# Delta rule with key and query norms folded into per-token factors, and decay rows spread by transfers from memory instead of products

## What is computed

```
q = repeat(l2norm(q), 2) * 128 ** -0.5      # 8 key heads of 128, 16 value heads
k = repeat(l2norm(k), 2)
gc    = cumsum(g)                            # per chunk of 64 tokens
decay = exp(gc[i] - gc[j])                   # j <= i
lhs   = eye + (beta_i k_i . k_j) * decay * (1 - eye)
u, w  = solve(lhs, v * beta), solve(lhs, k * beta * exp(gc))
attn  = (q_i . k_j) * decay
# per chunk: v_new = u - w S;  o = (q exp(gc)) S + attn v_new
#            S = S exp(gc_last) + (k exp(gc_last - gc))^T v_new
o = delta(forward) + reversed(delta(reversed inputs))
o = rms(o) * norm_w * silu(z);  y = o @ w_out
```

## Time and profile before

| | us |
|---|---|
| median of 3 runs | 1308.56 (1308.28 to 1309.36) |
| the profiled execution's own time | 1311.29 |
| its span in the profile | 1309.8 |
| PE busy | 1123.8 (86%) |
| DVE busy | 370.3 (28%) |
| ACT busy | 363.0 (28%) |
| POOL busy | 48.8 (4%) |
| mean granted clock of PE | 0.907 |

### The profile page before, as it was taken

The page is one execution under the profiler, slowest core; times in us unless marked ns, Lnnn a source line. Parts: engine busy times, 40 slices in busy tenths (PEclk is TensorE's granted clock), DMA queues, the critical chain, the costliest instruction groups (busy, mean ns, idle before and its releaser), DMA issues.

```text
span 1309.8 us, 23489 instructions
## 1 busy us (share of the span) xinstructions
PE 1123.8 (86%) x10332; PEld 852.1 (65%) x10332; DVE 370.3 (28%) x879; ACT 363.0 (28%) x902; POOL 48.8 (4%) x55
## 2 busy tenths in 40 slices
PE   6799999999889869767775979999997989996668
PEld 5577777777667654233332868888886877864457
DVE  1455655565442231000003124220002000614310
ACT  2345554655543111000003031120014011225220
POOL 1110010000000000000000000000000000400000
PEclk9799999999989969888886969999998998997559
DMA  5421221122011689999994224434441354430000
GB/s 209 185 100 66 91 75 67 67 92 74 35 66 65 280 367 407 420 421 421 422 421 193 97 100 146 159 111 147 161 160 65 101 189 115 177 129 1 0 1 33
DMA packets 35529, 210.55 MB, mean 161 GB/s; under 512 B 4688, under 2 KB 9168, under 8 KB 11488
## 3 DMA queue, kind: packets, MB, share of 16 engines
q1 hardware_dynamic: 35424, 209.00, 41.6%
HBM read 207.91 MB, written 1.08 MB: 160 GB/s over the span
## 4 chain that ended last, share of the span: by engine, by line
PE 72%; SPq 10%; DVE 6%; ACT 5%; DMA 4%; issue 2%; PEld 0%; PEldq 0%; ACTq 0%; DVEq 0%
PE ps L245 15%; SPq L230 10%; PE ps L397 10%; PE ps L1894 8%; PE ps L1812 4%; PE ps L400 4%; PE ps L698 2%; PE ps L709 2%; DMA arena<-in_wu 2%; PE ps L460 2%; PE ps L2225 2%; PE ps L426 2%; PE ps L445 2%; PE ps L261 1%; PE ps L1375 1%
## 5 line engine op out<-in xcount | busy, mean ns | idle before, releaser
L245 PE MATMUL ps<-slots,xt 128*128 128x256 f32 x640 | 139.1, 379 | 0.7 <-ACT xt L272 0.7
L397 PE MATMUL ps<-xt,slots 128*128 128x256 f32 x512 | 132.5, 407 | 2.0 <-DMA slots<-in_wu 2.0
L245 PEld LDWEIGHTS ps<-slots,xt 128*128 128x128 f32 x640 | 121.4, 190 | 17.8 <-ACT xt L272 1.1
L397 PEld LDWEIGHTS ps<-xt,slots 128*128 128x128 f32 x512 | 99.3, 202 | 26.7 <-issue 10.3
L1894 PE MATMUL ps<-slots,xt 128*128 128x256 f32 x512 | 110.7, 379 | 0.0
L1894 PEld LDWEIGHTS ps<-slots,xt 128*128 128x128 f32 x512 | 97.2, 190 | 13.2
L1375 PE MATMUL ps<-arena 128*32 128x512 f32 x304 | 48.9, 696 | 17.7 <-DMA arena<-in_wu 10.6
L400 PE MATMUL ps<-slots,arena 128*128 128x256 f32 x256 | 63.1, 389 | 0.0
L245 PE MATMUL ps<-slots,yt 128*128 128x256 f32 x256 | 57.8, 390 | 0.9 <-ACT yt L275 0.9
L1812 PE MATMUL ps<-xt,slots 128*128 128x256 f32 x256 | 58.1, 391 | 0.0
L989 DVE SCALAR_TENSOR_TENSOR arena<-arena 128x256 f32<-128x256 f32 x128 | 56.7, 489 | 0.3
(11 more groups left out here) (353 smaller groups left out, 1592.0 us busy)
## 6 DMA issues: line engine op xcount, KB each, us to landing
slots<-in_wu SPq DMA_DIRECT2D x120, 1024.0 KB, 4.9
arena<-in_wu SPq DMA_DIRECT2D x56, 1024.0 KB, 26.5
yt<-in_wu SPq DMA_DIRECT2D x10, 1024.0 KB, 26.2
arena<-bias_rows SPq DMA_DIRECT2D x1, 2048.0 KB, 15.6
arena<-in_xp SPq DMA_DIRECT2D x2, 512.0 KB, 4.4
xt<-in_xt SPq DMA_DIRECT2D x2, 512.0 KB, 9.2
x<-in_x SPq DMA_DIRECT2D x1, 1024.0 KB, 17.1
arena<-in_ln_g SPq DMA_DIRECT2D x2, 512.0 KB, 14.6
```

Source lines behind the costliest of these rows:

```text
L245: q = M.matmul(self.bank(cg, UC, t * UC), lhs[:, h * KT + k, t * P:(t + 1) * P], self.slot(s)[:, k, :], start=(t == 0 and k == 0 and h == ...
L397: q = M.matmul(bank(n, T), self.slots[:, s, k, n * P:(n + 1) * P], self.xt[:, k, :], start=(k == 0), stop=(k == KT - 1))
```

## The change

Four things are done at once.

1. Keys and queries stay unnormalised (`silu` writes them straight into `g.cv`). ACT squares them (`square`). `unit_sums` becomes four products with one column of ones, so that each token gets its sum on its own partition: 128x1 instead of 128x512.
2. The key norm goes into per-token numbers: `sums` (DVE) copies the sums, `unit` (ACT) takes the logarithm of two columns, `rates` (DVE) subtracts it from the logarithms of beta and decay, and `decay` and `scale_keys` use the result as bias and scale; `keep_v` scales the values by the key's length. The query norm goes into the epsilon of the output norm (`epsq`, `out_ln`).
3. The decay rows come by transfers: PE turns the summed gates once, ACT copies them (`g.crow`), SP stores them to a DRAM tensor `delta_rows` (two transfers), waits for that, and reads them back per head into `g.rowsb`, each row repeated over 64 partitions (two transfers a head). `decay_rows` and `spread` are gone.
4. `bars` waits for those transfers. `rates` waits for the logarithm on ACT.

```diff
@@ gdn_sync
         self.fill(0, U_GDN + 6)
+        SP.wait_ge(*g.cum_kept(1))
+        for x in range(2):
+            SP.dma_start(self.delta_rows[x].rearrange("c h (v i) -> (c h v) i", v=REP),
+                         g.crow[0:64, x * 64:(x + 1) * 64]).then_inc(*g.rows_out.up())
+        SP.wait_ge(*g.rows_out(2))
+
+        def rows_in(h):
+            for x in range(2):
+                SP.dma_start(g.rowsb[h % 2][g.halves[x]].rearrange("p (c n) -> p c n", c=4),
+                             self.delta_rows[x:x + 1, :, h, :].to_broadcast([P // 2, 4, P])).then_inc(
+                    *g.rows_in[h % 2].up())
+
+        rows_in(0)
+        rows_in(1)
         for h in range(QKH):
+            if h + 2 < QKH:
+                SP.wait_ge(*g.barred(h + 1))
+                rows_in(h + 2)
             self.fill(1, U_GDN + 3 * h + 4 if h + 1 < QKH else U_GOUT + 1)
@@ gdn_tensor
-        def decay_rows(h):
-            M.wait_ge(*g.spread(h + 1))
...
-            M.matmul(bank(2), c["together"], g.D[:, :, :, :].rearrange("p a b i -> p (a b i)"), start=True,
-                     stop=True).then_inc(*g.rows.up())
...
         def unit_sums(h):
+
             M.wait_ge(*g.squared(h + 1))
-            M.wait_ge(*g.barred(h + 1))
-            M.matmul(bank(2), c["ones"], g.sq[:, :, :].rearrange("p z t -> p (z t)"), start=True, stop=True).then_inc(
-                *g.unit_sums.up())
+            if h > 0:
+                M.wait_ge(*(g.sums_kept(1) if h == 1 else g.v_kept(h - 1)))
+            for cc in range(2):
+                for z in range(2):
+                    q = M.matmul(bank(2, 1, 2 * cc + z), g.sq[:, z, tile(cc)], c["ones"][:, 0:1], start=True, stop=True,
+                                 skip_group_check=True)
+            q.then_inc(*g.unit_sums.up())
...
         def keys(h):
             cv = g.cv[h % 3]
-            M.wait_ge(*g.unit(h + 1))
+            M.wait_ge(*g.qk_silu(h + 1))
...
-        decay_rows(0)
+        M.wait_ge(*g.gate_kept(1))
+        M.transpose(self.ps[0:64, 7, 0:P], g.cum[:, :, :, :].rearrange("p c w h -> p (c w h)"), ident).then_inc(
+            *g.cum_turned.up())
...
-            if ahead:
-                decay_rows(h + 1)
@@ gdn_scalar
         def silu(h):
             A.wait_ge(*g.qk_conv(2 * h + 2))
-            A.activation(g.cn[:, 0:2], g.cn[:, 0:2], ACT.Silu).then_inc(*g.qk_silu.up())
+            if h > 2:
+                A.wait_ge(*g.reads(3 * (h - 3) + 3))
+            for cc in range(2):
+                q = A.activation(g.cv[h % 3][:, :, cc * P:(cc + 1) * P].rearrange("p z (x i) -> p z x i", x=2),
+                                 self.chunks(g.cn[:, 0:2], cc), ACT.Silu)
+            q.then_inc(*g.qk_silu.up())
+
+        def square(h):
+            A.wait_ge(*g.qk_silu(h + 1))
+            if h > 0:
+                A.wait_ge(*g.unit_sums(h))
+            A.activation(g.sq[:, :, :], g.cv[h % 3][:, :, :], ACT.Square).then_inc(*g.squared.up())
...
         def unit(h):
 
             n = h - 3
-            A.wait_ge(*g.unit_sums(h + 1))
-            if h > 0:
-                A.wait_ge(*g.unit(h))
+            A.wait_ge(*g.sums_kept(h + 1))
             A.preload_act_table_set("natural_log_exp_and_others")
-            A.activation(g.rn[:, :, :], two(2), ACT.Ln, bias=col(0)).then_inc(*g.norm_ln.up())
+            A.activation(g.lnk[:, h], g.kss[:, h], ACT.Ln, bias=col(0)).then_inc(*g.norm_ln.up())
...
+            A.wait_ge(*g.rated(h + 1))
+            ss = g.rates[:, h, :, 2:4, :]
+            A.activation(ss, ss, ACT.Exp).then_inc(*g.rates_made.up())
@@ gdn_vector
         def bars(h):
-            V.wait_ge(*g.rows(h + 1))
+            V.wait_ge(*g.rows_in[h % 2](2 * (h // 2) + 2))
...
+        def sums(h):
...
+            V.wait_ge(*g.unit_sums(h + 1))
+            both = bank(2, 4).rearrange("p (c z) -> p c z", c=2)
+            V.tensor_copy(g.kss[:, h], both[:, :, 1])
+            V.tensor_scalar(g.epsq[:, h], both[:, :, 0], 1e-6 * HD, 1e-12 * HD, ALU.mult, ALU.add).then_inc(
+                *g.sums_kept.up())
+
+        def rates(h):
+            V.wait_ge(*g.norm_ln(h + 1))
+            V.tensor_tensor(g.rates[:, h], g.logs[:, :, :, 2 * h:2 * h + 2],
+                            g.lnk[:, h].unsqueeze(2).unsqueeze(3).to_broadcast([P, 2, 4, REP]), ALU.subtract).then_inc(
+                *g.rated.up())
...
         bars(0)
-        squares(0)
-        apply_unit(0)
+        sums(0)
+        rates(0)
         triangles(0)
```

More of the change, by code:

```diff
@@ L286, in gdn @@
         g.g, g.lb = al("g", [P, 2, 2, VH]), al("lb", [P, 2, 2, VH])
-        g.cum, g.egc, g.neg, g.bias, g.ss = (al(n, [P, 2, 2, VH]) for n in ("cum", "egc", "neg", "bias", "ss"))
+        g.cum, g.egc, g.neg = (al(n, [P, 2, 2, VH]) for n in ("cum", "egc", "neg"))
+        g.logs, g.rates = al("logs", [P, 2, 4, VH]), al("rates", [P, QKH, 2, 4, REP])
+        g.lnk, g.invk, g.epsq, g.kss = (al(n, [P, QKH, 2]) for n in ("lnk", "invk", "epsq", "kss"))
+        g.crow = al("crow", [P, P])
+        g.rowsb = [al(f"rows{b}", [P, 512]) for b in range(2)]
         g.eg = al("eg", [P, 2, 2, 2, VH])
@@ L311, in gdn @@
             new("SP", n, 16) for n in ("gate_inputs_in", "xt_in", "common_in", "delta_constants_in", "x_in"))
-        (g.gates, g.sums, g.rows, g.q_done, g.v0_done, g.z0_done, g.unit_sums, g.v_turned, g.keys, g.o_turned,
+        g.rows_out = new("SP", "decay_rows_out", 16)
+        g.rows_in = [new("SP", f"decay_rows{b}_in", 16) for b in range(2)]
+        (g.gates, g.sums, g.cum_turned, g.q_done, g.v0_done, g.z0_done, g.unit_sums, g.v_turned, g.keys, g.o_turned,
          g.ys, g.zx, g.zw, g.reads, g.us, g.avs, g.adds) = (
-            new("PE", n) for n in ("gates", "gate_sums", "decay_rows", "q_projected", "v0_projected", "z0_projected",
+            new("PE", n) for n in ("gates", "gate_sums", "decays_turned", "q_projected", "v0_projected", "z0_projected",
                                    "unit_sums", "v_turned", "keys", "out_turned", "y_product",
@@ L332, in gdn @@
         g.compact = new("ACT", "blocks_compact")
-        g.cleared2, g.spread, g.masked = (new("POOL", n) for n in ("w_cleared", "gates_spread", "level_masked"))
+        g.cleared2, g.masked = (new("POOL", n) for n in ("w_cleared", "level_masked"))
         self.gdn_sync(g)
@@ L839, in keep_v @@
             A.wait_ge(*g.v_turned(h + 1))
-            A.activation(g.vtm[h % 2][:, :, :, :].rearrange("p c v e -> p (c v e)"), bank(2), ACT.Copy).then_inc(
-                *g.v_kept.up())
+            A.wait_ge(*g.norms(h + 1))
+            for cc in range(2):
+                q = A.activation(g.vtm[h % 2][:, cc].rearrange("p v e -> p (v e)"), bank(2, 256, cc * 256), ACT.Copy,
+                                 scale=g.invk[:, h, cc:cc + 1])
+            q.then_inc(*g.v_kept.up())
         def keep_k(h):
@@ L862, in out_ln @@
             A.wait_ge(*g.out_squares(4 * h + 4))
-            A.activation(g.ost[:, :], g.ost[:, :], ACT.Ln, scale=1.0 / HD, bias=col(0)).then_inc(*g.out_ln.up())
+            for cc in range(2):
+                o = g.ost[:, 2 * cc:2 * cc + 2]
+                q = A.activation(o, o, ACT.Ln, scale=1.0 / HD, bias=g.epsq[:, h, cc:cc + 1])
+            q.then_inc(*g.out_ln.up())
         def out_exp(h):
@@ L914, in gdn_scalar @@
                 silu(h + 1)
+                square(h + 1)
             if step:
@@ L1164, in gdn_vector @@
             if ahead:
-                squares(h + 1)
+                sums(h + 1)
             if step:
@@ L1168, in gdn_vector @@
                 out(h - 1, 1)
+            if ahead:
+                rates(h + 1)
             if level:
@@ L1225, in gdn_gpsimd @@
         G.wait_ge(*g.gate_kept(1))
-        spread(0)
-        spread(1)
         for h in range(QKH):
@@ L1230, in gdn_gpsimd @@
                 mask(h, l)
-                if l == 1 and h + 2 < QKH:
-                    spread(h + 2)
     def moe(self):
```

70 lines of the change are left out of this document (24 added, 46 removed).

## The result

| | before | after |
|---|---|---|
| median of the runs, us | 1310.39 (6 runs) | 1318.86 (6 runs, 1315.8 to 1321.39) |
| ratio, 95% interval | | 1.0065 (1.0047 to 1.0083) |
| the profiled execution's own time, span | 1311.29, 1309.8 | 1318.45, 1317.0 |
| mean granted clock of PE | 0.907 | 0.902 |

The change makes the kernel slower, by 8.5 us in this comparison. A second one, made later with the same two kernels on one chip, gave 1319.09 against 1312.86, ratio 1.0044 (1.003 to 1.0057). By the two ratios the cost is 5.8 to 8.5 us, where 4.2 were forecast.

A forecast was written before the change was run, and what follows sets the result against it. PE was taken to bound the loop, the path over ACT and DVE the start. Terms: -6.0 + 0 + 0 + 10.2 = +4.2 us, so 1312.8 against the median 1308.56; range 1307.8 to 1317.0.

The forecast's parts named there:

- term 4: Start: the decay rows' transfers queue behind a fill, so `triangles(0)` and the first level come 10.2 us later (5.5 to 14.1).
- Term 1: Loop: dropping the decay product L409 saves PE 0.86 us a turn, 6.0 us in seven turns.
- Term 2: Loop: four one-column products cost PE 0.87 us, as much as the 512-column product they replace (0.86); nothing saved.
- Rival (b): Sums on PE: one-column products cost next to nothing; at nothing the sum is -1.8 us, 1306.8; chance 0.08.
- Term 3: Loop: new waits between PE, DVE and ACT delay the value's taps 2.1 us but cost PE nothing.
- Rival (c): Loop: the logarithm's chain is one table load longer, PE waits 0.4 us a turn, 3.0 in all: 1315.8; chance 0.13.
- The slack that I called thin: Loop: first rows of `left` end near 240.2, PE wants them at 241.08; 0.85 us of slack.
- Rival (a): Start: the rows' transfers overtake the fill, delay 5.5 us, sum -0.5, 1308.1, not slower; chance 0.12.
- (d): Start: neither loss nor gain, because the rows arrive before PE's projection ends; excluded by SP's list, no chance given.
- (e): Start and sums: rows overtake the fill and sums are cheap, -6.5 us, 1302.1; chance 0.05 together with anything unforeseen.
- The signs set beforehand: Start and loop: reads land at 51.5 to 54, PE idles about 18 us, first level near 62, turn about 42.7.
- The low clock: Start: PE's clock, at 0.50, expected back 6.3 us after PE restarts, as before, despite the longer pause.

The follow-up runs named there:

- norms alone: The change's norms and one-column sums only, decay rows made by POOL and PE as before: 1312.43 us against 1311.62 for the kernel before, ratio 1.0007.
- the first experiment: The changed kernel with both stores moved ahead of two weight fills and the first reads right behind those: 1306.83 us against 1313.06 before the change, ratio 0.996.
- the larger pieces: The changed kernel with sums sorted by head, so each read takes 2 KB per partition, not four of 512 B: 1316.09 us against 1312.86 before, ratio 1.0035.

## Why the prediction was right in direction and too small

The forecast was 4.2 us slower, 1312.8 with a range up to 1317.0. The time was 1318.86, outside and 6.1 more. Of these, 1.8 us are the base (1310.39 beside the change, 1308.56 in the runs shown at first); of the other 4.2, term 4 is 2.7 in the first profile, and the rest lies within what the clock and the parts behind the loop vary by.

- **Term 1, the decay product: right.** A turn takes 42.75 in place of 43.58, 0.83 saved where 0.86 was forecast. The loop as a whole took 262.9 to 264.6 in the ten other profiles of kernels with the rows by transfer, against 269.8: 5.2 to 6.9 less, mostly 6, where 6.0 were forecast. In the first profile of the change it was 265.3, only 4.5 less, by the clock in turn 0 and the gap in turn 4.
- **Term 2, the sums: right.** 3.46 against 3.43 us in place, and norms alone make no difference. The row of 0.109 us a record was the right one: L530's eight records take 0.92 us until the next product starts (241.39 to 242.31), 0.115 each. Rival (b), whose one-column products cost next to nothing, falls.
- **Term 3, the waits: right.** No new wait of PE in 243 us of the loop. Rival (c) falls. The slack that I called thin held.
- **Rival (a), the rows overtake the fill:** falls, with the 17.2 us of the store that was issued early. (d) was excluded by SP's list, and is what the first experiment made by editing that list. (e) falls with (a) and (b).
- **Term 4, the start: the mechanism right, the size wrong.** Forecast 10.2, measured 12.9 in the first profile and 12.5 in the second. By its steps, from `unit_sums(0)` on: the stores land at 7.6 by forecast and at 8.5 and 8.4 by measurement, since they come behind the fill, which itself took 7.9 and 7.8 us where the earlier trace rows has 7.2. The reason given for the 7.2 was too large: of the 7 MB issued before that fill most had been moved by 41.9. The rates of 393 to 442 GB/s until 47.0 leave about 2 MB for it and what was ahead, an estimate, so about 1 MB ahead. From there to `bars(0)` I had 3.2 us (0.65 for issue, 2.5 under way); it took 5.4 and 5.1. Behind that I had 5.3, and it took 4.9. **The step that failed is the read.** I priced 128 KB, repeated over 64 partitions in pieces of 512 B, between two small transfers of 3.3 and 1.6 us. A read took 0.65 to issue, where I had 0.33, and in the chain shown above the second landed 4.65 us behind the start of its issue, where I had 2.5. So the step was 2.2 and 1.9 us too small, of the 2.7 and 2.3 that the term missed. The size of a transfer alone did not tell this; the way it is cut did, as the larger pieces show, with which the same step took 3.55. The 2.0 us of the sentence on the Trainium skill (DMA: Bandwidth & Descriptors, Anatomy of one DMA) are given there for transfers that POOL issues; these come from SP, and their reads took 3.7 to 4.65.
- **The signs set beforehand: met, in part by luck.** `bars(0)` starts at 53.20 (51.5 to 54 was named) and the first level at 62.41 (near 62). Both are counted from the start of the execution, and there `unit_sums(0)` came 2.4 us earlier than in the kernel before, for reasons shown above that the forecast doesn't have. That hid the 2.7 us by which term 4 was short. PE's idle time shows it: 21.3 us where about 18 were named.
- **The low clock.** PE's clock stayed at 0.50 for 6.4 us after the first level began in the change, and 6.3 before, which I had expected. That they agree was luck: the second profile of the change has 3.4, and the other kernels 3.0 to 5.8, with idle times of 4.4 to 21 us ahead of that level in no order with it. So a microsecond or two of every comparison of two profiles is this.

With the start as measured, 12.7 in the mean, and the usual 6.1 of the loop, the sum is 6.6 us; with the 4.5 of the loop in the first profile it is 8.4 (12.9 - 4.5). The two comparisons gave 8.5 and, by the ratio 1.0044, 5.8.

## What to carry to other kernels

Moving work from a full engine to a transfer pays only what the transfer's place in its queue allows: here the swap saved 6 us in the loop and lost 13 in a start that happens once, and moving the stores and the first reads up in SP's list turned 0.4 to 0.65% slower into 0.4% faster. So before such a change, find the first consumer of the first transfer, and count what stands ahead in the queue, in bytes that are under way and in statements that wait. Price a transfer that repeats a short row over partitions by how it is cut and not only by its bytes, and where it is waited for lay the source out so that a partition reads one piece. Where the rows come in time, the layout is worth nothing.

## What the hardware showed that I had not expected

- Two reads of 128 KB took 5.1 to 5.4 us in 256 pieces of 512 B each, for the most part at 85 to 89 GB/s and a share of the transfer engines of about a third, and 3.55 us in 64 pieces of 2 KB each, at 168 to 184.
- A store of 16 KB landed 0.4 to 0.5 us behind the last load issued ahead of it: 2.2 us after its issue behind one fill that was nearly through, 17.2 behind 7 MB, of which about 1 MB had been moved when it was issued (an estimate from the rates until then).
- The rest of `gdn` behind the loop took 110.3 us at a mean granted clock of 0.97 and 112.5 at 0.94, in kernels that differ only in the start (transfers early, and the change).
- The stages that no edit touched took 877 or 880 us, in two executions of one kernel. A gain of 3 us in a stage can't be read from the span of one profile; it can from the stretch itself.
